# adaLN weights in a two-layer backbone step: 16 of 40 pieces between layer 0's projections, their rows transposed by VectorE

## The chip, the cores and the metric

One core of a Trainium2 chip runs the whole step. The metric is the device time of one execution in microseconds, median of three runs.

## The reference

```python
D_MODEL = 1024; SEQ = 128; DEC_SEQ = 512; DEPTH = 2
def modulation(cvec, w_mod, b_mod):
    m = jax.nn.silu(cvec) @ w_mod + b_mod            # 1024 -> 6 x 1024
    return jnp.split(m[..., None, :], 6, axis=-1)
...
  h = x * (1 + scale1) + shift1                      # adaLN, from c (512 latent tokens) or c_ctx (128 context tokens)
  p = h @ w_in[l]                                    # 1024 -> 3088: q, k, v; gated DeltaNet; HGRN2
  x = LayerNorm(alpha * x + gate1 * (concat(A, B, C) @ w_out[l]))
  x = LayerNorm(alpha * x + gate2 * FFN_l(x * (1 + scale2) + shift2))
```

Each layer needs six vectors of 1024 for each of the two groups, that is, two rows (from c and c_ctx) times a 1024 x 6144 matrix. Only shift1 and scale1 of layer 0 are needed for its projections; the others are read behind its attention.

## The kernel before

The five engines run programs of their own, and semaphores join them. All of w_mod is 48 pieces of 1024 x 256, 1 MB each. Eight of them (layer 0's shift1 and scale1) are loaded first into regions of their own. The other 40 pass through the ring `wbuf`, three slots of 1 MB that SP fills strictly in the order of `weight_plan()`; w_in's pieces pass through the same ring.

**A piece.** `mod_piece_job` on TensorE multiplies it: 8 products over the contraction, with two useful columns of 32 (c and c_ctx) as weights, spread over four groups of 32 PSUM rows. A float32 product is two PE instructions, 16 to a piece. So the piece leaves four partial sums for each of the two rows, at PSUM rows 32q and 32q + 1. `mod_row` on ScalarE copies the 128 x 256 block to `modrow` (four pieces wide). When four are there, `mod_turn` transposes and adds the four partial sums at once: per 128 columns of `modrow` one product with `modrow` as weights and the 128 x 2 matrix `sel` as moving data. `mod_chunk` on VectorE adds the bias and writes `modT`. After the pieces of gate2 of layer 1, `gate_rows` writes those as rows (2 x 1024), which go to memory.

**A piece of w_in** (qa0, qa1, kv, f0, f1, b0, b1, b2, gb, ba, i, gc, qc, in this order) is used in halves of float16. ScalarE's `upper` scales it in its slot (line 1028) and writes the upper half (line 1031), the latter only once the piece two before it, whose region it takes, has been used by TensorE. GpSimd's `lower` (line 804) subtracts and writes the lower half. Only that counts up `w_lo`, on which TensorE's job waits and on which SP's `freed` waits before it refills the slot; a slot that held a piece of w_mod is free when its product is done (`ps_full`). ScalarE calls `upper` for a piece at fixed places between its reads of TensorE's results: f0 behind q3, f1 behind va, b0 and b1 behind f0 and f1, b2 behind b1, gb behind b3, i behind b5, gc behind gb1, qc behind i.

**Order.** The jobs of TensorE take the four PSUM slots in turn, in the order of `psum_plan()`: q0 to q3, ka, va, f0, f1 (each in two parts, a and b), b0 to b5, gb0, gb1, ba, ia, ib, kout, ckt, five rotations `rot`, gc0, gc1, qc0, the first two scores, qc1, and then the attention loop of 20 units x. In unit x TensorE makes the scores of x + 2, transposes the probabilities of x, multiplies two pieces of w_mod, makes the output of x - 1 and, in every second unit, a turn. VectorE makes the scores' maxima of x + 2 and divides x + 1; ScalarE copies the transposed probabilities, exponentiates and copies the output. The rotary products wait for ScalarE's copies of kout and ckt, and VectorE's three operations per rotation run beside GpSimd's `lower` of qc.

```python
                elif what.startswith("mod"):
                    bank, turn = PS[f"{l}.mp{what[3:]}"]
                    sp.wait_ge(ps_full[bank], turn + 1)
                else:
                    sp.wait_ge(sg["w_lo"], SPLIT[f"{l}.{what}"] + 1)
```

Of the kernel before, what the change touches and what calls it, by code (L numbers as in the profile page):

```python
# [55 lines left out]
_WIDTH = [("ident", P), ("sel", 2), ("blk", P), ("rot", P), ("rev", 2 * P), ("am", 5 * P), ("tie", 64), ("mean", 1), ("tile", 17),  # L56
          ("gap", 4), ("hg", 2 * 8 * P), ("room", 2 * 8 * P), ("cos", LAT), ("sin", LAT),
# [10 lines left out]
def constant_table():  # L68
# [50 lines left out]
    put("sel", np.stack([i % 32 == g for g in range(2)], 1))  # L119
# [12 lines left out]

def mod_pieces(x):

    return (2 * x, 2 * x + 1)
# [17 lines left out]
def psum_plan():  # L153
# [4 lines left out]
    for l in range(DEPTH):  # L158
# [3 lines left out]
        j += ["gc0", "gc1", "qc0", "S" + units[0], "S" + units[1], "qc1"]  # L162
        for x in range(len(units)):
# [7 lines left out]
            if l == 0 and x % 2:  # L171
                j.append("*mt" + str(x // 2))
                j += ["g2r"] * (x == 17)
# [48 lines left out]
def weight_plan():  # L222
# [41 lines left out]
def backbone_kernel(nc, x_prompt, x_sample, cache_k, cache_v, state_gdn, state_hgrn, c, c_ctx, w_mod, b_mod, w_in,  # L264
# [12 lines left out]
    with ctx:  # L277
# [142 lines left out]
        rtmp, siluc, g2row = mem(spare, 1024, LAT), mem(spare, 1536, 48), mem(extra, 0, D)  # L420

# [593 lines left out]
        def _(act):  # L1015
# [26 lines left out]
            def mod_row(l, i):  # L1042
                j = f"{l}.mp{i}"
                copy(modrow[:, (i % 4) * 256:(i % 4 + 1) * 256], L.full(j)[:, 0:256], j)


# [13 lines left out]
                       (wr[:, :, :], moe_router[0].rearrange("(k p) e -> p k e", p=P))]  # L1060
            assert len(par_in) == PAR_DMAS
# [4 lines left out]
            for i in range(4):  # L1066
                mod_row(0, i)
# [5 lines left out]
            for i in range(4, 8):  # L1073
                mod_row(0, i)
# [7 lines left out]
            for l in range(DEPTH):  # L1082
# [102 lines left out]
                for x, (n, t) in enumerate(units):  # L1185
# [3 lines left out]
                    if l == 0:  # L1189
                        for i in mod_pieces(x):  # L1190
                            mod_row(*mod_piece(i))
# [7 lines left out]
                    if l == 0 and x == 17:  # L1199
# [457 lines left out]
        def _(dve):  # L1657
# [26 lines left out]
            L.done("par")  # L1684

# [562 lines left out]
        def _(pe):  # L2248
# [107 lines left out]
            for l in range(DEPTH):  # L2356
# [6 lines left out]
                for t in range(2, 4):  # L2363
                    project(l, "qa1", J(f"q{t}"), (t % 2) * P, h2)
# [705 lines left out]
```

## Time and profile before

| | |
|---|---|
| median of 3 runs | 2442.57 us (2441.56 to 2445.93) |
| profiled execution | 2446.07 us, span 2444.3 us, mean granted clock 0.937 |
| PE / DVE / ACT / POOL busy | 2141.7 / 1470.8 / 1284.5 / 758.5 us |
| HBM read / written | 368.35 / 29.11 MB |

Busy times are those of whole engines over stages with different limits; PEld is TensorE's loading of weights. Line 2268 is the helper through which nearly all of TensorE's products go, lines 1662, 1666 and 1670 are VectorE's helpers, and 1020 is ScalarE's copy, so instructions are told apart by their tiles and shapes: `ps<-wbuf,const 128*32 128x256` is the product of a w_mod piece, `ps<-const,modrow 128x2` the turn, `ps<-hT,arena 128x512` a projection job. Line 2475 transposes the probabilities, one group for each unit. SPq is SP's queue of DMA issues. PEclk is the granted clock of TensorE, 1.00 being 2.4 GHz. A row of the windows view gives the stretch, its length, the busy time (x instructions) of PE, PEld, DVE, ACT and POOL, PEclk, the DMA engines' mean share and GB/s. A row of the groups view gives busy us and mean ns of one, then the idle time before them and what ended it.

### The profile page before, as it was taken

What the parts mean: (1) busy time and instruction counts of PE and PEld (TensorE: products, weight loads), DVE (VectorE), ACT (ScalarE), POOL (GpSimd) and SP (SyncE); (2) the same over time, 40 slices, a digit from 0 to 9 for tenths busy, and PEclk for the clock granted to TensorE, in tenths of its full rate; (3) what the DMA queues carried; (4) which work ended last, traced back from release to release, by engine and by line L of the source; (5) the groups of instructions that cost most, each with busy time, mean ns of one, the idle gap of its engine ahead of it and who ended that gap; (6) DMA issues with size and microseconds to landing.
All of it is one profiled execution on the core that took longest, in us unless ns stands there. A gap on an engine that the chain in (4) does not pass through costs nothing.

```text
span 2444.3 us, 54596 instructions
## 1 busy us (share of the span) xinstructions
PE 2141.7 (88%) x23078; PEld 1337.8 (55%) x23078; DVE 1470.8 (60%) x1822; ACT 1284.5 (53%) x1664; POOL 758.5 (31%) x557
## 2 busy tenths in 40 slices
PE   5998987878989999999898878888969999999990
PEld 4765656755565555555765557654544444444440
DVE  3155745559362121214558666486379999999976
ACT  3443753446444242423443764466268787787862
POOL 0432115432314342423232135333123333332321
PEclk8999998888999999999999888889979999999995
DMA  9322990020212222215221000020276677980023
GB/s 277 105 81 76 298 302 11 3 56 4 72 53 72 84 82 73 86 68 162 86 89 38 1 10 3 3 57 22 97 257 207 233 266 275 332 314 35 27 104 137
DMA packets 215386, 278.46 MB, mean 114 GB/s; under 512 B 28178, under 2 KB 188798, under 8 KB 215040
## 3 DMA queue, kind: packets, MB, share of 16 engines
q1 hardware_dynamic: 203776, 243.60, 30.8%
q0 software_dynamic: 8432, 29.89, 3.3%
q8 instruction: 166, 2.72, 0.5%
q10 hardware_dynamic: 2959, 1.83, 0.3%
q14 instruction: 53, 0.43, 0.1%
HBM read 368.35 MB, written 29.11 MB: 163 GB/s over the span
## 4 chain that ended last, share of the span: by engine, by line
PE 52%; issue 16%; DVE 14%; POOL 7%; ACT 6%; DMA 3%; SPq 1%; POOLq 0%; DVEq 0%; ACTq 0%
PE ps L2268 50%; POOL mix L968 5%; DVE arena L1662 2%; DMA wbuf<-in_w_mod 1%; DVE mix L1670 1%; PE ps L2475 1%; DVE xT L1662 1%; DVE const L1662 1%; ACT arena L1142 1%; DVE mix L1662 1%; DVE mix L1666 1%; DVE yg L1662 1%; DVE arena L1666 1%; DVE hT L1662 1%; POOL mix L971 1%
## 5 line engine op out<-in xcount | busy, mean ns | idle before, releaser
L2268 PE MATMUL ps<-hT,mix 128*128 128x512 f16 (+2 forms) x3024 | 377.5, 287 | 24.7 <-DVE hT L1662 15.3
L2268 PE MATMUL ps<-w,xgT 128*128 128x512 f16 x1632 | 365.4, 381 | 7.0 <-DVE w L2163 7.0
L2163 DVE SCALAR_TENSOR_TENSOR w<-wst,w 128x2048 f16<-128x2048 f32 x136 | 309.8, 2317 | 22.8 <-ACT w L1523 22.6
L2268 PEld LDWEIGHTS ps<-hT,mix 128*128 128x128 f16 x3024 | 228.2, 99 | 172.4 <-issue 17.1
L1000 POOL TENSOR_TENSOR a<-aval,a 128x256 f16<-128x256 f32 x68 | 159.1, 2340 | 370.8 <-ACT a L1571 370.8
L2268 PEld LDWEIGHTS ps<-w,xgT 128*128 128x128 f16 x1632 | 157.1, 98 | 185.8 <-issue 10.2
L1523 ACT ACTIVATE w<-wst 128x2048 f16<-128x2048 f32 x136 | 251.5, 1899 | 6.6 <-DMA xs_rows<-htok,slot_i 6.5
L2268 PE MATMUL ps<-mix 128*128 128x512 f16 (+5 forms) x1856 | 204.5, 288 | 14.5 <-POOL mix L971 8.8
L2268 PE MATMUL ps<-hT,arena 128*128 128x128 f16 (+1 forms) x1440 | 201.2, 302 | 1.0 <-DVE const L1662 1.0
L2268 PE MATMUL ps<-w2m,aT 128*128 128x512 f16 x816 | 188.6, 381 | 5.6 <-DVE aT L2201 5.6
L2268 PEld LDWEIGHTS ps<-mix 128*128 128x128 f16 (+3 forms) x1856 | 121.3, 124 | 88.7 <-POOL mix L971 12.4
L2169 DVE SCALAR_TENSOR_TENSOR w2m<-wst,w2m 128x2048 f16<-128x2048 f32 x68 | 155.8, 2291 | 15.8 <-ACT w2m L1531 15.2
L2127 DVE SCALAR_TENSOR_TENSOR mix<-ps,mix 128x640 f32<-128x640 f32 x22 | 18.1, 825 | 239.4 <-PE ps L2268 239.4
L804 POOL TENSOR_TENSOR arena<-wbuf,arena 128x2048 f16<-128x2048 f32 x24 | 100.0, 4166 | 196.1 <-ACT arena L1031 196.0
L2268 PEld LDWEIGHTS ps<-hT,arena 128*128 128x128 f16 x1440 | 112.0, 98 | 88.3 <-issue 5.8
L968 POOL TENSOR_TENSOR mix<-wbuf,mix 128x2048 f16<-128x2048 f32 x33 | 134.2, 4081 | 57.0 <-ACT mix L1475 57.0
L2268 PEld LDWEIGHTS ps<-w2m,aT 128*128 128x128 f16 x816 | 79.8, 98 | 103.1 <-DVE aT L2201 6.4
L2268 PE MATMUL ps<-arena 64*32 64x32 f32 (+5 forms) x4320 | 104.4, 220 | 34.0 <-issue 20.3
L1531 ACT ACTIVATE w2m<-wst 128x2048 f16<-128x2048 f32 x68 | 129.4, 1903 | 0.2 <-PE ps L2268 0.2
L971 POOL TENSOR_TENSOR mix<-mix 128x640 f16<-128x640 f32 x22 | 30.7, 1396 | 258.2 <-ACT mix L1484 258.2
L2134 DVE TENSOR_TENSOR arena<-arena,ps 128x640 f32<-128x640 f32 x80 | 65.6, 821 | 73.7 <-PE ps L2268 73.7
L2268 PEld LDWEIGHTS ps<-arena 64*32 64x32 f32 (+3 forms) x4320 | 70.3, 117 | 66.9 <-issue 43.5
(360 smaller groups left out, 3625.0 us busy)
## 6 DMA issues: line engine op xcount, KB each, us to landing
wst<-in_moe_w SPq DMA_DIRECT2D x204, 1024.0 KB
wbuf<-in_w_mod SPq DMA_DIRECT2D x40, 1024.0 KB
wbuf<-in_ffn_w SPq DMA_DIRECT2D x33, 1024.0 KB
wbuf<-in_w_in SPq DMA_DIRECT2D x20, 1024.0 KB
xs_rows<-in_table SPq DMA_DIRECT2D x17, 512.0 KB, 6.3
ys_rows<-yb POOLq DMA_DIRECT2D x17, 512.0 KB, 4.0
wbuf<-in_w_out SPq DMA_DIRECT2D x32, 256.0 KB
xg<-xs_rows POOLq DMA_DIRECT2D x16, 512.0 KB, 5.7
```

The source lines that it names most:

```text
L804: L.do(g.tensor_tensor(split_parts(what)[1], wpiece(WP[f"{l}.{what}"][0], n), split_parts(what)[0], ALU.subtract), "w_lo")
L968: g.tensor_tensor(v[1], wpiece(j), v[0], ALU.subtract).then_inc(sg["w_lo"], 1)
L971: g.tensor_tensor(a2[1][:, t], gbuf[:, t], a2[0][:, t], ALU.subtract).then_inc(sg["a_lo"], 1)
L1000: g.tensor_tensor(a16[:, s % 2, 1, :], aval[:, s % 2, :], a16[:, s % 2, 0, :], ALU.subtract).then_inc(sg["m_alo"], 1)
L1523: a.activation(quarter(s, p)[0], staged(s, p), ACT.Copy, scale=WS).then_inc(sg["m_hi13"], 1)
L1531: a.activation(w2p[s % 2][0], staged(s, 2), ACT.Copy, scale=WS).then_inc(sg["m_hi2"], 1)
L1662: ins = v_.tensor_tensor(o, x, y, op)
L1666: ins = v_.tensor_scalar(o, x, s1, s2, op0, op1)
L2134: v_.tensor_tensor(yacc[:, m], yacc[:, m], ps[:, b, 0:NT], ALU.add).then_inc(ps_free[b], 1)
L2163: v_.scalar_tensor_tensor(out=q[1], in0=staged(s, p), scalar=WS, in1=q[0], op0=ALU.mult, op1=ALU.subtract).then_inc(sg["m_lo13"], 1)
L2169: v_.scalar_tensor_tensor(out=q[1], in0=staged(s, 2), scalar=WS, in1=q[0], op0=ALU.mult, op1=ALU.subtract).then_inc(sg["m_lo2"], 1)
L2268: return mm_(o, w, x, start=first, stop=last, skip_group_check=True)
```

## The change

- 16 of the 40 pieces get a place in the projections of layer 0 (`MOD_AT`: behind q3, ka, va, f0, f1, b0 to b5, gb0, gb1, i, ckt and gc0), four turns with them (`TURN_AT`). SP fetches them between the pieces of w_in (`MOD_FETCH`). The 24 others are spread over the 20 units, 6 to five units, and their six turns are at `TURN_UNIT`.
- `mod_row` moves from ScalarE to VectorE and becomes a transpose of 32x32 blocks, for all 48 pieces. After it the two rows are columns: in block k of 32 columns they stand at columns 32k and 32k + 1.
- A turn becomes four products, one for each group of 32 output rows, with the wider `sel` (128 x 32) as weights and 16 columns of `modrow` as moving data, in place of eight. `gate_rows` becomes 32 products of 32 columns in place of two of 512.
- `sel` is loaded by a DMA of its own on ScalarE's queue.

```diff
+MOD_AT = {j: i for i, j in enumerate(("q3", "ka", "va", "f0b", "f1b", "b0", "b1", "b2", "b3", "b4", "b5", "gb0", "gb1", "ib",
+                                     "ckt", "gc0"))}
+TURN_AT = {"f1b": 0, "b3": 1, "gb1": 2, "qc0": 3}
+MOD_FETCH = {"f0": (0,), "f1": (1, 2), "b0": (3,), "b1": (4, 5), "b2": (6, 7), "ba": (8, 9), "i": (10, 11), "gc": (12,),
+               "qc": (13, 14, 15)}
+TURN_UNIT = {3: 4, 6: 5, 9: 6, 13: 7, 16: 8, 19: 9}
...
 def mod_pieces(x):
 
-    return (2 * x, 2 * x + 1)
+    return tuple(range(16 + 6 * x // 5, 16 + 6 * (x + 1) // 5))
...
-        j += ["gc0", "gc1", "qc0", "S" + units[0], "S" + units[1], "qc1"]
+        j += ["gc0", "gc1", "qc0"]
+        if l == 0:
+            j = [y for x in j for y in [x] + [f"*mt{TURN_AT[x]}" for _ in "1" if x in TURN_AT]
+                 + [f"*mp{MOD_AT[x]}" for _ in "1" if x in MOD_AT]]
...
-        names += [f"{l}.{x}" for x in j]
+        for x in j:
+            names.append(f"{l}.{x}")
+            if l == 0 and x in MOD_FETCH:
+                names += ["%d.mod%d" % mod_piece(i) for i in MOD_FETCH[x]]
         if l == 0:
-            for i in range(40):
+            for i in range(16, 40):
...
-            def mod_row(l, i):
-                j = f"{l}.mp{i}"
-                copy(modrow[:, (i % 4) * 256:(i % 4 + 1) * 256], L.full(j)[:, 0:256], j)
...
+            o, n = CONST_AT["sel"]
+            par_in.append((sel, table[:, o:o + n]))
...
-            mod_chunk(0, 0)
-            mod_chunk(0, 1)
+            def chunk_of(k):
+                lm, i = mod_piece(4 * k)
+                mod_chunk(lm, i // 4)
+
+            def mod_row(l, i):
+                j = f"{l}.mp{i}"
+                L.free(v_.transpose(modrow[:, (i % 4) * 256:(i % 4 + 1) * 256], L.full(j)[:, 0:256]), j)
+
+            def row_of(job):
+                mod_row(*mod_piece(MOD_AT[job]))
+
+            for c in range(2):
+                for i in range(4):
+                    mod_row(0, 4 * c + i)
+                L.done("par")
+                mod_chunk(0, c)
...
                     modulate(l, 0, 8)
+                    for job in ("q3", "ka", "va"):
+                        row_of(job)
...
+                if l == 0:
+                    row_of("f0b")
                 L.done(J("f1b"))
                 if l == 0:
+                    chunk_of(TURN_AT["f1b"])
+                    row_of("f1b")
...
                 for t in range(6):
+                    if l == 0:
+                        if t == 3:
+                            chunk_of(TURN_AT["b3"])
+                        row_of(f"b{t}")
                     L.done(J(f"b{t}"))
+                    if l == 0 and t == 5:
+                        row_of("gb0")
+                        chunk_of(TURN_AT["gb1"])
+                        row_of("gb1")
...
-                    if l == 0 and x % 2:
-                        lm, i = mod_piece(2 * (x - 1))
-                        mod_chunk(lm, i // 4)
+                    if l == 0:
+                        for i in mod_pieces(x):
+                            mod_row(*mod_piece(i))
+                        if x in TURN_UNIT:
+                            chunk_of(TURN_UNIT[x])
...
                 L.done(f"{l}.mp{4 * c + 3}")
-                for k in range(KT):
-                    ins = mm(s[:, 2 * k:2 * k + 2], modrow[:, k * P:(k + 1) * P], cst("sel"))
+                part = modrow.rearrange("p (k a i) -> p a k i", a=4, i=32)
+                for q in range(4):
+                    ins = mm(s[32 * q:32 * q + 32, 0:16], sel, part[:, q, :, 0:2])
                 close(ins, f"{l}.mt{c}")
 
             def gate_rows():
 
                 s = open_("0.g2r")
-                for h in range(2):
-                    ins = mm(s[0:2, h * 512:h * 512 + 512], cst("sel"), modrow[:, h * 512:h * 512 + 512])
+                for k in range(32):
+                    ins = mm(s[0:2, k * 32:k * 32 + 32], modrow[:, k * 32:k * 32 + 2], sel)
...
+                def mods_at(job):
+                    if l:
+                        return
+                    if job in TURN_AT:
+                        lm, i = mod_piece(4 * TURN_AT[job])
+                        mod_turn(lm, i // 4)
+                    if job in MOD_AT:
+                        mod_piece_job(*mod_piece(MOD_AT[job]))
+
                 for t in range(2, 4):
                     project(l, "qa1", J(f"q{t}"), (t % 2) * P, h2)
+                mods_at("q3")
                 project(l, "kv", J("ka"), 0, h2)
+                mods_at("ka")
```

The order of SP's loads, from the load of f0 on. Rows with `in_w_in` are pieces of w_in, 128x2048 is a table. Before:

```order
L700 DMA wbuf<-in_w_in 128x8x256 [waits w_lo] x5
L643 DMA const<-in_table 128x2048 [waits ps_full2]
L700 DMA wbuf<-in_w_in 128x8x256 [waits w_lo]
L700 DMA wbuf<-in_w_in 128x8x16 [waits w_lo]
L700 DMA wbuf<-in_w_in 128x8x256 [waits w_lo] x3
```

and with the change, as far as the load of b2, the table and two pieces behind them:

```order
L716 DMA wbuf<-in_w_in 128x8x256 [waits w_lo]
L716 DMA wbuf<-in_w_mod 128x8x256 [waits w_lo]
L716 DMA wbuf<-in_w_in 128x8x256 [waits w_lo]
L716 DMA wbuf<-in_w_mod 128x8x256 [waits w_lo]
L716 DMA wbuf<-in_w_mod 128x8x256 [waits ps_full1]
L716 DMA wbuf<-in_w_in 128x8x256 [waits w_lo]
L716 DMA wbuf<-in_w_mod 128x8x256 [waits ps_full3]
L716 DMA wbuf<-in_w_in 128x8x256 [waits ps_full1]
L716 DMA wbuf<-in_w_mod 128x8x256 [waits w_lo]
L716 DMA wbuf<-in_w_mod 128x8x256 [waits ps_full0]
L716 DMA wbuf<-in_w_in 128x8x256 [waits w_lo]
L659 DMA const<-in_table 128x2048 [waits ps_full2]
```

The pieces of w_mod (M0 to M15 in the order of their use) now take slots between those of w_in: M0 behind f0; M1, M2 behind f1; M3 behind b0; M4, M5 behind b1; M6, M7 behind b2 and the table; M8, M9 behind gb and ba; M10, M11 behind i; M12 behind gc; M13, M14, M15 behind qc.

TensorE from the job va (128x128, 120 products) to turn 0. Before:

```order
L2268 MATMUL ps<-arena,hT 128x128 [waits ps_free2,w_lo]
L2268 MATMUL ps<-arena,hT 128x128 x119
L2268 MATMUL ps<-arena,hT 128x256 [waits ps_free3,w_lo]
L2268 MATMUL ps<-arena,hT 128x256 x95
L2268 MATMUL ps<-arena,hT 128x256 [waits ps_free0]
L2268 MATMUL ps<-arena,hT 128x256 x23
```

and with the change, from M1 on:

```order
L2308 MATMUL ps<-wbuf,const 32x256 [waits ps_free3,w_full0]
L2308 MATMUL ps<-wbuf,const 32x256 x7
L2308 MATMUL ps<-arena,hT 128x128 [waits ps_free0,w_lo]
L2308 MATMUL ps<-arena,hT 128x128 x119
L2308 MATMUL ps<-wbuf,const 32x256 [waits ps_free1,w_full1]
L2308 MATMUL ps<-wbuf,const 32x256 x7
L2308 MATMUL ps<-arena,hT 128x256 [waits ps_free2,w_lo]
L2308 MATMUL ps<-arena,hT 128x256 x95
L2308 MATMUL ps<-arena,hT 128x256 [waits ps_free3]
L2308 MATMUL ps<-arena,hT 128x256 x23
L2308 MATMUL ps<-wbuf,const 32x256 [waits ps_free0,w_full0]
L2308 MATMUL ps<-wbuf,const 32x256 x7
```

Each product of a piece stands in TensorE's queue between two projection jobs and waits there for its own transfer (`w_full`).

## Rows read from the trace of the kernel before

**Rows 1.** Windows view, five stretches: length, then the columns as told above.
```profile
71.20:193.80 122.60, 122.60 (x1131) 86.47 (x1132) 43.56 (x41) 50.98 (x49) 43.20 (x14) 0.99 0.32 101
239.30:268.80 29.50, 25.71 (x267) 16.79 (x267) 19.70 (x41) 20.40 (x44) 2.87 (x8) 0.88 0.86 273
268.80:304.10 35.30, 35.30 (x385) 24.88 (x385) 26.19 (x60) 25.99 (x56) 4.73 (x10) 1.00 0.93 296
304.10:335.20 31.10, 30.28 (x352) 21.01 (x350) 17.92 (x50) 19.71 (x50) 3.16 (x10) 0.95 0.99 314
335.20:371.50 36.30, 29.38 (x284) 17.51 (x283) 8.88 (x38) 14.57 (x45) 4.48 (x13) 0.84 0.79 254
```

**Rows 2.** Waits of PE, 239.3 to 371.5 us: total us, times, longest.
```profile
PE ps L2268 <- DMA wbuf<-in_w_mod: 8.1, 8, 2.4
PE ps L2475 <- DVE arena L1666: 5.8, 2, 4.2
```

**Rows 3.** Groups by form, 0 to 380 us: busy us, mean ns | idle before.
```profile
L2268 PE MATMUL ps<-wbuf,const 128*32 128x256 f32 x640 | 45.3, 421 | 8.1 <-DMA wbuf<-in_w_mod 8.1
L2268 PE MATMUL ps<-const,modrow 128*128 128x2 f32 x192 | 26.6, 269 | 1.0 <-ACT modrow L1020 0.9
L1020 ACT ACTIVATE modrow<-ps 128x256 f32<-128x256 f32 x48 | 18.4, 383 | 41.2 <-PE ps L2268 40.6
```

**Rows 4.** Timeline of PE, ACT and SP, 84 to 125 us: start, us.
```profile
84.23 6.68 PE L2268 MATMUL ps<-hT,arena 128*128 128x512 f16 x48
84.49 0.70 ACT L1020 ACTIVATE arena<-ps 128x640 f32<-128x640 f32 x1 [5.82 <-PE ps L2268]
90.75 33.06 PE L2268 MATMUL ps<-arena,hT 128*128 128x128 f16 x360
93.32 0.39 SPq L700 DMA_DIRECT2D wbuf<-in_w_in  x1
97.70 0.70 ACT L1020 ACTIVATE va<-ps 128x640 f32<-128x640 f32 x1 [6.00 <-PE ps L2268]
```

**Rows 5.** GB/s in 40 slices: 92 to 102, then 105 to 121 us.
```profile
GB/s 0 0 0 0 0 0 0 0 0 29 49 147 168 266 295 352 385 393 385 389 385 389 340 172 115 0 0 0 0 0 0 0 0 0 0 0 0 0 0 0
...
GB/s 0 0 0 0 0 0 31 97 248 356 384 374 381 392 463 407 430 410 430 410 389 82 0 0 0 0 0 0 0 0 0 0 0 0 0 0 0 0 56 108
```

**Rows 6.** Timeline at the rotations, 193 to 206 us, PE and DVE.
```profile
198.44 4.54 PE L2268 MATMUL ps<-arena,const 128*128 128x512 f32 x6 [2.79 <-ACT koutb L1020]
198.56 4.43 DVE L1662 TENSOR_TENSOR arena<-arena,const 128x512 f32<-128x512 f32 x1
```

**Rows 7.** Timeline of PE around 240 us, then its window to 243.7.
```profile
232.26 1.93 PE L2268 MATMUL ps<-wbuf,const 128*32 128x256 f32 x32
239.29 0.87 PE L2475 MATMUL ps<-const,arena 128*128 128x128 f32 x6 [4.24 <-DVE arena L1666]
240.10 3.60 PE L2268 MATMUL ps<-wbuf,const 128*32 128x256 f32 x32
...
240.00:243.70 3.70, 3.70 (x36) 1.55 (x36) 2.85 (x9) 1.19 (x2) 0.00 (x0) 0.54 0.38 103
```

**Rows 8.** Timeline of PE, short float32 products at 391 us.
```profile
391.14 1.15 PE L2268 MATMUL ps<-arena,extra 64*64 64x64 f32 x32 [0.85 <-ACT arena L1249]
```

**Rows 9.** Timeline of PE, the second turn of the prologue.
```profile
37.44 2.29 PE L2268 MATMUL ps<-const,modrow 128*128 128x2 f32 x16 [0.66 <-ACT modrow L1020]
```

**Rows 10.** Timeline of DVE in a unit of the attention loop.
```profile
277.03 1.23 DVE L1670 SCALAR_TENSOR_TENSOR arena<-ps,const 128x1024 f32<-128x1024 f32 x1 [0.51 <-PE ps L2268]
278.29 1.22 DVE L1858 TENSOR_REDUCE small<-arena 128x2 f32<-128x1024 f32 x1
...
283.29 1.23 DVE L1670 SCALAR_TENSOR_TENSOR arena<-ps,const 128x1024 f32<-128x1024 f32 x1 [0.89 <-PE ps L2268]
```

**Rows 11.** Groups of DVE by form, 0 to 380 us.
```profile
L1666 DVE TENSOR_SCALAR arena<-ps 128x256 f32<-128x256 f32 x4 | 1.7, 425 | 4.1 <-PE ps L2268 4.1
L1790 DVE RECIPROCAL lbt<-extra 128x512 f32<-128x512 f32 x1 | 3.4, 3353 | 0.0
```

More of the change, by code:

```diff
@@ L53 @@
 OFF_BA, OFF_F, OFF_I, OFF_QC, OFF_GC, OFF_GB, OFF_B, OFF_KV = 1792, 1808, 2320, 2576, 2832, 1536, 768, 512
-_WIDTH = [("ident", P), ("sel", 2), ("blk", P), ("rot", P), ("rev", 2 * P), ("am", 5 * P), ("tie", 64), ("mean", 1), ("tile", 17),
-          ("gap", 4), ("hg", 2 * 8 * P), ("room", 2 * 8 * P), ("cos", LAT), ("sin", LAT),
+_WIDTH = [("ident", P), ("skip", 2), ("blk", P), ("rot", P), ("rev", 2 * P), ("am", 5 * P), ("tie", 64), ("mean", 1), ("tile", 17),
+          ("gap", 4), ("hg", 2 * 8 * P), ("room", 2 * 8 * P), ("cos", LAT), ("sin", LAT), ("sel", 32),
           ("zero", D), ("near", 2 * 6 * 32), ("wide", 4 * 2 * 64), ("first", 3 * 64)]
@@ L118, in constant_table @@
     put("tie", np.broadcast_to((e[None, :] < e[:, None]).reshape(1, 64), (P, 64)))
-    put("sel", np.stack([i % 32 == g for g in range(2)], 1))
+    put("sel", np.stack([i % 32 == g for g in range(32)], 1))
     put("tile", np.broadcast_to(np.arange(MT).reshape(1, MT), (P, MT)))
@@ L161, in psum_plan @@
         j += ["gb0", "gb1", "ba", "ia", "ib", "kout", "ckt"] + [f"rot{t}" for t in range(5)]
-        j += ["gc0", "gc1", "qc0", "S" + units[0], "S" + units[1], "qc1"]
+        j += ["gc0", "gc1", "qc0"]
+        if l == 0:
+            j = [y for x in j for y in [x] + [f"*mt{TURN_AT[x]}" for _ in "1" if x in TURN_AT]
+                 + [f"*mp{MOD_AT[x]}" for _ in "1" if x in MOD_AT]]
+        j += ["S" + units[0], "S" + units[1], "qc1"]
         for x in range(len(units)):
@@ L170, in psum_plan @@
                 j.append("O" + units[x - 1])
-            if l == 0 and x % 2:
-                j.append("*mt" + str(x // 2))
-                j += ["g2r"] * (x == 17)
+            if l == 0 and x in TURN_UNIT:
+                j.append("*mt" + str(TURN_UNIT[x]))
+                j += ["g2r"] * (x == 16)
             j += SIDE.get(x, [])
@@ L1065, in _ @@
                                 L.full("cT")[:, 0:16].rearrange("p (g k) -> p g k", g=2), ACT.Silu), "cT")
-            for i in range(4):
-                mod_row(0, i)
             s = L.full("par")
@@ L1072, in _ @@
             upper(0, "qa0")
-            for i in range(4, 8):
-                mod_row(0, i)
             tokens_in(0)
@@ L1198, in _ @@
                     side(x)
-                    if l == 0 and x == 17:
+                    if l == 0 and x == 16:
                         copy(g2row[0:2, :], L.full("0.g2r")[0:2, :], "0.g2r")
@@ L1833, in _ @@
                 stt(SP, ZA, -1.0, ZA, ALU.mult, ALU.max, to="ab_in")
+                if l == 0:
+                    row_of("ib")
+                    row_of("ckt")
                 dve.wait_ge(sg["rope_in"], 16 * (l + 1))
@@ L1840, in _ @@
                     tt(qk[:, t, 0:LAT], qk[:, t, 0:LAT], rtmp, ALU.add, to="rope_ready")
+                if l == 0:
+                    row_of("gc0")
+                    chunk_of(TURN_AT["qc0"])
                 def scores(x):
@@ L1905, in _ @@
                         divide(x + 1)
-                    if l == 0 and x % 2:
-                        lm, i = mod_piece(2 * (x - 1))
-                        mod_chunk(lm, i // 4)
+                    if l == 0:
+                        for i in mod_pieces(x):
+                            mod_row(*mod_piece(i))
+                        if x in TURN_UNIT:
+                            chunk_of(TURN_UNIT[x])
                     side(x)
@@ L2379, in _ @@
                 tokens(J("va"), w, (P, 256), range(TT))
+                mods_at("va")
                 for p_ in ("f0", "f1"):
@@ L2391, in _ @@
                 tokens(J("ib"), w, (0, 256), range(4, 5))
+                mods_at("ib")
                 L.done(J("ka"))
@@ L2402, in _ @@
                     project(l, "gc", J(f"gc{t}"), t * P, h2)
+                    mods_at(f"gc{t}")
                 project(l, "qc", J("qc0"), 0, h2)
+                mods_at("qc0")
                 L.need("rope_ready", 5)
@@ L2481, in _ @@
                         output(x - 1)
-                    if l == 0 and x % 2:
-                        lm, i = mod_piece(2 * (x - 1))
+                    if l == 0 and x in TURN_UNIT:
+                        lm, i = mod_piece(4 * TURN_UNIT[x])
                         mod_turn(lm, i // 4)
-                    if l == 0 and x == 17:
+                    if l == 0 and x == 16:
                         gate_rows()
```

11 lines of the change are left out of this document (6 added, 5 removed).

## The prediction

> **What bounds the kernel now.** I first cut the span by the busy time of each engine in stretches [rows 1]. From 71.2 to 193.8 us, layer 0's projections, PE is busy in all of 122.6 us at a granted clock of 0.99 while DMA is used for 0.32 of the time. From 239.3 to 371.5 us, the attention loop, PE is still busy 88 to 100% of three of the four stretches, but DMA is at 0.86 to 0.99: the 40 pieces of w_mod pass here, two to a unit. Then I asked for the waits [rows 2]: in the whole loop PE idles only 8.1 us for w_mod and 5.8 us for VectorE. So the loop is not bound by DMA alone: most of what the pieces cost is PE's own time, 45.3 us for 40 products (1.13 us each) and 26.6 us for 12 turns (2.2 each) [rows 3]. Moving a piece to the projections moves its product from one busy stretch of PE to another and gains nothing by itself. The gain must come from the shorter turns and the waits; what the move breaks is the supply of weights.
>
> I count against the profiled execution, 2446.07 us with a span of 2444.3; the median of the three runs is 2442.57, 3.5 lower. I take the difference that I work out and put it on the median. About 0.2%, 4.9 us, is what a measurement of this kernel can tell from no change.
>
> **The projections, product by product.** M0 to M15 are the moved products. A pair of products takes 1.93 us at full clock [rows 7], so 16 take 15.5 us, and PE has no idle time there to hide them in: +15.5. Four short turns replace nothing here. One is 8 PE instructions; the nearest row has 32 short ones in 1.15 us [rows 8], 0.29 for 8, the lower end; the long turn's 2.2 is the upper. I take 0.4, near the short row: +1.6.
>
> Now the waits. The ring wbuf has three slots and SP fills them strictly in order. A slot of a w_in piece comes free only when POOL has written its lower half. For f0 the row of the trace is: PE begins the job after q3 at 84.23, ACT reads q3 at 84.49, then splits f0, POOL subtracts, and SP issues at 93.32 [rows 4]: **9.1 us from the end of the PE job to the issue**. The transfer starts then; the bandwidth line goes to zero at 98.25, 4.9 us after the issue, and with two transfers in line 7.3 us after it [rows 5], so 2.4 for each further one. A projection job takes 6.5 us (84.23 to 90.75), a half of f 13.2 (33.06 for va and the two halves; va ends some 0.3 before ACT reads it at 97.70, so it is 6.7) [rows 4]. With the SP order of the change:
> - M1 sits in the slot of f0, freed 9.1 after q3. It lands at 14.0; PE asks after M0 and ka, 1.0 + 6.5. Wait 6.5.
> - M3 stands behind b0, and b0 takes the slot of f1, freed 9.1 after va: 16.4 against M2 and f0, 14.1. Wait 2.3.
> - M6 stands behind b2 and the 1 MB table load; the slot is b1's, freed 9.1 after f1: 18.8 against turn 0, M4, b0, M5, b1, 15.4. Wait 3.4.
> - M9 sits in the slot of gb, freed 9.1 after b3: 14.0 against turn 1, M8 and b4, 7.9. Wait 6.1.
> - M12 stands behind gc, in the slot of i, freed 9.1 after b5: 16.4 against 15.4. Wait 1.0.
>
> The other eleven come in time by the same sums. Together +19.3. Behind a waiting M stands everything of PE; the weights' chain through ACT and POOL is released by PE's jobs, so it is late as well and gives nothing back.
>
> The clock. After 4.24 us of idle PE ran a pair of products in 3.60 instead of 1.93 us, at a granted clock of 0.54 in that stretch [rows 7]: almost all of it at the lower level, 1.2 GHz. That is 1.7 us lost per such idle. M1, M6 and M9 give idles of that size: +5.1. (Lower end 0; upper end in the rivals.)
>
> Around the rotations M13 and M14 fall into a wait that PE has anyway, 2.79 us for ACT's koutb copy [rows 6]: -1.9. But VectorE comes to the rotations later against POOL's 4 us subtraction, and its product of two SBUF operands took 4.43 us there [rows 6]; the second rotation's bank comes free about 1.5 us later: +1.5. In the prologue the turn of chunk 1 stands on the path, 2.29 us [rows 9], now 0.4, and the table for it adds one small DMA: -1.7 with the transpose's 0.2 over the copy counted in. ScalarE loses 48 copies of 383 ns [rows 3]; it waited for PE before 40.6 us of them, so that is worth nothing here. The prologue's rows now wait on VectorE for tab_in, but w_mod for them lands later than that anyway (PE's turn of [rows 9] comes at 37.44, right behind the last of them).
>
> Sum: 15.5 + 1.6 + 19.3 + 5.1 - 0.4 - 1.7 = **+39.4 us**.
>
> **The attention loop.** Unit 0 has one piece less, -1.1. For the rest I take each stretch of [rows 1] twice: PE's busy time less the pieces (1.13) and turns that go, and VectorE's busy time plus 0.03 for each instruction (277.03 + 1.23 to 278.29 in [rows 10]) plus 0.45 for each transpose. A transpose is not in the trace. A 128x256 operation from PSUM takes 425 ns, the slowest kind of instruction 3.35 us for 512 columns [rows 11], 1.7 for 256: I take 0.42 and a gap, the nearest row. (The Trainium skill, Vector Engine (DVE) Microarchitecture Reference, 3.8, has the transpose sustain one element per cycle and lane, which at the 0.96 GHz of VectorE: DVE Perf Modes, Specifications, is an estimate of 0.27 us; by it the loop would gain 3 us more.)
> - 239.3 to 268.8, units 1 to 4, 8 pieces become 5, two turns one: PE 18.3, VectorE 19.7 + 1.2 + 2.3 = 23.2. They hand work to each other, I take 25.0: -4.5.
> - 268.8 to 304.1, units 5 to 9, 10 become 6, three turns two: PE 25.0, VectorE 26.2 + 1.8 + 2.7 = 30.7: -4.6. **VectorE becomes the bound.** In a unit of 6.26 us it has only 0.89 us idle even now [rows 10].
> - 304.1 to 335.2: PE 21.8, VectorE 22.1; 23.0: -8.1.
> - 335.2 to 371.5: PE 29.4 - 4.5 - 5.8 = 19.1, plus 1.0 because the gate rows become 64 short instructions (64 x 0.036 = 2.3 at least, at a long turn's 2.2 / 16 = 0.14 apiece 8.8 at most; I take 2.9 against 1.9), plus 1.0 of waits; 21.1: -15.2. Here the w_mod waits of [rows 2] go, since 6 pieces for five units leave DMA ahead.
>
> Sum: **-33.5 us**. Net +5.9 us, 2446.07 to 2452.0, on the median **2448.5 us**.
>
> **Rivals.**
> 1. VectorE's transposes fall into its idle time and PE alone sets the loop. For: it idles in every unit [rows 10]. Against: the idle is 0.9 us and operand hand-overs use it. PE 18.3 + 25.0 + 21.8 + 20.1 and the 5.8 us of [rows 2] make 91.0 instead of 132.2, with unit 0 -42.3; net -2.9, 2439.7. Chance 0.24.
> 2. The pieces land before PE asks, because the issue comes sooner than 9.1 us after the job. Then the 19.3 and the 5.1 fall away: net -18.5, **2424**, faster. It decides at M1: if it lands within 7.5 us of q3. Against: [rows 4] has ACT and POOL in a row between. Chance 0.10.
> 3. The clock falls at all five new waits and stays low twice as long: 5 x 3.4 instead of 5.1, +11.9, 2460. For: the row of 0.54 came after a wait of just this kind of length. Against: two of the five are shorter than 2.5 us, and the projections around them are dense. This is also what the Trainium skill, TensorE: Matmul & The Clock Gate, "HAM oscillation", says against this change: DMA waits between matmuls put the array back on the lower clock each time; by that rule the time is this rival's 2460, and the row of 0.54 agrees with it. Chance 0.12.
> 4. The transpose runs like the slowest instruction, 1.7 us: 1.25 more for each of 17 in the first three stretches, where VectorE is the bound, +21, 2470. Against: no arithmetic in it. Chance 0.07.
>
> The forecast itself has 0.47, with a range of its own from 2441 to 2455. That the change doesn't take place is excluded by the instruction order.
>
> **How the numbers follow.** Faster by over 4.9 us: rival 2 and a third of rival 1, 0.18. Same: most of the rest of rival 1 and a third of the forecast, 0.29. Slower: 0.53. The range 2433 to 2462 holds the forecast, rival 1 with the loop 7 us better than I make it, and rival 3; it leaves out rivals 2 and 4.
>
> **What would show it.** Right: PE waits for wbuf before the products after ka and after b4, 5 to 7 us each, and shorter ones after f0 and b1; the first score of layer 0 some 39 us later than at 222.5; a granted clock under 0.99 in the projections; in the loop VectorE over 85% busy in units 5 to 9, and hardly a w_mod wait; the first product of the next stage within some 6 us of 371.5. Wrong: no wait at the product after ka, or a transpose far from 0.4 us, or the loop from unit 1 on no longer than rival 1's 91 us, where I forecast 132.2 - 32.4 = 99.8.

## The result and the profile after

| | before | after |
|---|---|---|
| median (4 runs each, side by side) | 2442.07 us | **2478.39 us** (2477.10 to 2480.81) |
| ratio, 95% interval | | 1.0147 [1.0131, 1.0163] |
| profiled execution, span | 2446.07, 2444.3 | 2477.10, 2475.3 |
| PE / DVE / ACT busy | 2141.7 / 1470.8 / 1284.5 | 2131.5 / 1493.6 / 1266.0 |

Slower, as forecast, but by 36 us where 6 were forecast, and outside the range. The times here and below are those of fast executions: one of e7 (3643.69 us) and one of e8 (3610.20 us), both at a mean granted clock of 0.55, are left out. In the changed kernel lines 2308, 2535, 1668, 1672, 1036 and 820 are what 2268, 2475, 1662, 1666, 1020 and 804 were; 1789 is the transpose of a row.

I laid four landmarks of PE beside each other: the start of `q2` (71.17 before), the first score of layer 0 (222.47), the first product of the stage behind the loop (371.51) and the end of the span.

| from, to | before | after | difference | forecast |
|---|---|---|---|---|
| start to `q2` | 71.2 | 70.3 | -0.9 | -1.7 |
| `q2` to the first score | 151.3 | 202.7 | +51.4 | +41.1 |
| first score to the end of the loop | 149.0 | 123.5 | -25.5 | -33.5 |
| behind the loop | 2072.8 | 2078.8 | +6.0 | 0 |

First the projections: waits of PE from 70.3 to 273.0 us (total us, times, longest), and in PE's timeline the rows at the first two of them; the last four rows are SP's queue of DMA issues.

```profile
PE ps L2308 <- DMA wbuf<-in_w_mod: 24.4, 5, 6.9
PE ps L2308 <- ACT koutb L1036: 1.3, 1, 1.3
```

```profile
83.41 1.07 PE L2308 MATMUL ps<-wbuf,const 128*32 128x256 f32 x16
84.42 6.69 PE L2308 MATMUL ps<-hT,arena 128*128 128x512 f16 x48
97.69 1.94 PE L2308 MATMUL ps<-wbuf,const 128*32 128x256 f32 x16 [6.58 <-DMA wbuf<-in_w_mod]
99.56 8.81 PE L2308 MATMUL ps<-arena,hT 128*128 128x128 f16 x120
108.31 1.07 PE L2308 MATMUL ps<-wbuf,const 128*32 128x256 f32 x16
127.06 1.50 PE L2308 MATMUL ps<-wbuf,const 128*32 128x256 f32 x16 [4.48 <-DMA wbuf<-in_w_mod]
...
92.40 1.02 SPq L716 DMA_DIRECT2D wbuf<-in_w_mod  x2
117.30 0.39 SPq L716 DMA_DIRECT2D wbuf<-in_w_in  x1
117.73 0.58 SPq L716 DMA_DIRECT2D wbuf<-in_w_mod  x1
118.36 1.22 SPq L716 DMA_DIRECT2D wbuf<-in_w_in  x1
```

`q3` ends where M0 starts, at 83.41; SP issues M1 at 92.40, 9.0 us later ([rows 4] gave 9.1), and PE stands still for it until 97.69. Before the change no product waited there. Behind the wait M1 takes 1.94 us and the job after it 8.81 us, where the same forms take 1.07 and (in [rows 4]) about 6.7. The granted clock from 97.7 to 107.0 us is 0.68. The five waits are 6.58, 4.48, 4.23, 6.91 and 2.22 us, before M1, M3, M6, M9 and M12, the very five of the forecast.

Then the loop, cut at the same units as [rows 1] (windows view, columns as there), and its waits (answering to [rows 2]).

```profile
289.80:316.30 26.50, 21.14 (x195) 13.22 (x195) 21.93 (x44) 17.71 (x37) 5.33 (x8) 0.78 0.53 169
316.30:351.30 35.00, 28.47 (x288) 18.40 (x288) 29.07 (x66) 21.82 (x43) 4.07 (x10) 0.95 0.57 183
351.30:375.80 24.50, 21.78 (x267) 15.07 (x263) 20.43 (x53) 15.92 (x41) 3.78 (x10) 1.00 0.68 218
375.80:396.50 20.70, 15.79 (x248) 9.71 (x246) 11.63 (x43) 10.70 (x34) 4.39 (x13) 1.00 0.74 239
```

```profile
PE ps L2308 <- DVE modrow L1789: 9.0, 5, 3.4
PE ps L2535 <- DVE arena L1672: 6.1, 2, 5.1
PE ps L2535 <- DVE modrow L1789: 3.7, 4, 2.1
PE ps L2535 <- ACT arena L1036: 3.0, 1, 3.0
PE ps L2308 <- DMA wbuf<-in_w_mod: 1.3, 1, 1.3
```

```profile
L1789 DVE STREAM_TRANSPOSE modrow<-ps 128x256 f32<-128x256 f32 x48 | 21.6, 450 | 101.7 <-PE ps L2308 100.8
L2308 PE MATMUL ps<-modrow,const 128*32 128x16 f32 x96 | 3.2, 196 | 10.4 <-DVE modrow L1789 10.4
```

The waits for w_mod are nearly gone (1.3 for 8.1) and twelve turns take 3.2 us for 26.6 [rows 3]. In their place PE waits 12.7 us for VectorE's transposed rows: 9.0 at the turns and 3.7 for PSUM banks that only the transpose sets free. Units 5 to 9 take 35.0 us, as long as before with four pieces more.

### The profile page after: what moved, and what is told of

It reads as the page before. It is cut to its first block, busy times and chain, and to the rows that moved or that the text cites. A ratio compares the mean times of both kernels' runs of the same rounds, so it can differ in the third digit from the quotient of the medians.

```text
span 2475.3 us, 54524 instructions
## 1 busy us (share of the span) xinstructions
PE 2131.5 (86%) x23042; PEld 1321.5 (53%) x23042; DVE 1493.6 (60%) x1870; ACT 1266.0 (51%) x1616; POOL 755.4 (31%) x557
## 4 chain that ended last, share of the span: by engine, by line
PE 47%; DVE 17%; issue 16%; POOL 8%; ACT 7%; DMA 3%; SPq 1%; POOLq 0%; DVEq 0%; ACTq 0%
PE ps L2308 45%; POOL mix L984 5%; DVE arena L1668 2%; DMA wbuf<-in_w_mod 2%; DVE mix L1676 1%; DVE arena L1672 1%; DVE mix L1668 1%; POOL arena L820 1%; DVE xT L1668 1%; ACT arena L1151 1%; DVE const L1668 1%; DVE mix L1672 1%; DVE hT L1668 1%; DVE yg L1668 1%; SPq L716 1%
## 5 line engine op out<-in xcount | busy, mean ns | idle before, releaser
L2308 PEld LDWEIGHTS ps<-mix 128*128 128x128 f16 (+3 forms) x1856 | 122.3, 125 | 90.4 <-POOL mix L987 12.4
L987 POOL TENSOR_TENSOR mix<-mix 128x640 f16<-128x640 f32 x22 | 30.7, 1397 | 258.2 <-ACT mix L1490 258.2
```

Of the source, the lines that this page charges most:

```text
L987: g.tensor_tensor(a2[1][:, t], gbuf[:, t], a2[0][:, t], ALU.subtract).then_inc(sg["a_lo"], 1)
L2308: return mm_(o, w, x, start=first, stop=last, skip_group_check=True)
```

## The experiments

The runs came in three groups, e1 to e4, e5 to e8 and e9 to e11. The kernel before, run beside each group, had medians of 2446.17, 2445.63 and 2443.49 us; ratios are against it, and kernels of different groups are compared by their distance from it. Four theories were at hand: the waits in the projections with the clock behind them (W, C), VectorE's rows (V), and, for the 6 us behind the loop, where no instruction had changed, the place of the code in PE's program (Q) or chance. The diffs show the lines that matter; calls on VectorE that only follow a moved job are left out.

### e1: the rows without the move

```diff
-MOD_AT = {"q3": 0, "ka": 1, ... "gc0": 15}
+MOD_AT = {}
-    return tuple(range(16 + 6 * x // 5, 16 + 6 * (x + 1) // 5))
+    return (2 * x, 2 * x + 1)
```

> No piece is moved: all 40 stay in the attention loop, and only the transposing by VectorE and the four short products are kept. Theory W (what the change lost is the waits for w_mod tiles among the projections, 24 us, and the lower clock behind them, about 10 us): without moved pieces both are gone, the first score starts within 1 us of where it did before the change, and the loop's turns give back some of 26.6 us of PE time less the waits for VectorE's rows (13.5 us in the changed kernel with 24 pieces, so 15 to 22 us with 40): 2430 to 2440. Rival V (VectorE's rows themselves are the loss, by the PSUM banks and turns that they hold up): slower than before, 2450 or more. Rival H (the 5 us that appeared behind the loop belong to the new code): 2445.

Measured: **2449.81 us, 1.0023 [1.0005, 1.0041]**. W's 2430 to 2440 is missed, and V's 2450 nearly met. The waits among the projections are gone (first score at 218.27, 4.2 us earlier than before the change, 2.4 of them ahead of the projections), yet the loop takes 152.9 us against 149.0 and ends at 371.15, where it ended before (371.51). The waits of that loop, and the window of its last units, say why:

```profile
PE ps L2286 <- DMA wbuf<-in_w_mod: 11.2, 7, 2.9
PE ps L2286 <- DVE modrow L1787: 8.6, 9, 2.0
PE ps L2286 <- ACT arena L1034: 2.2, 1, 2.2
PE ps L2513 <- DVE modrow L1787: 2.1, 1, 2.1
```

```profile
263.70:371.20 107.50, 87.66 (x1013) 53.38 (x1014) 67.03 (x178) 48.46 (x117) 11.94 (x32) 0.88 0.85 273
```

PE is busy for 122.6 us of that loop instead of 133.2, so the turns do save 10.6 us; the waits for w_mod rise from 8.1 to 11.2 and those for rows from 0.3 (behind ScalarE's copies) to 10.7. What PE saves it spends waiting, in part for weights (DMA at 0.85 in the later units), in part for VectorE. That short turns pay only if pieces leave the loop is argued from this, not shown: no run has all 40 pieces there with the rows ahead of the division (e3). What e1 loses against the kernel before lies behind the loop (2082.5 us for 2072.8), where theory H had put something; e9 returns to it.

### e2: the move with long turns

```diff
-                L.free(v_.transpose(modrow[...], L.full(j)[:, 0:256]), j)
+                L.free(v_.tensor_copy(modrow[...], L.full(j)[:, 0:256]), j)
-                for q in range(4):
-                    ins = mm(s[32 * q:32 * q + 32, 0:16], sel, part[:, q, :, 0:2])
+                for k in range(KT):
+                    ins = mm(s[:, 2 * k:2 * k + 2], modrow[:, k * P:(k + 1) * P], sel[:, 0:2])
```

> The pieces move as in the change, but the rows are copied by VectorE without a transpose and turned by the eight long products (and two for the gate rows) of the kernel before. Theory W: the waits for w_mod tiles stay as they are, 24 to 26 us, the turns cost about 1.7 us more each, ten in all, and the waits of PE for VectorE's rows stay, since a copy of the same tile is as long (425 ns in the row of before): 2478 + 17 = 2490 to 2497. Rival V (the transposes are what VectorE is late with): the waits for rows vanish, 13.5 us, and the time is 2478 to 2484.

Measured: **2491.71 us, 1.0201 [1.0167, 1.0235]**. W's number. In the loop PE waits 9.6 and 1.3 us for rows that are merely copied (424 ns each against 450 for the transpose), so V as a matter of the transpose falls: it is the hand-over to VectorE that costs, whatever VectorE does to the row. The w_mod waits were 19.9 us, less than the 24 to 26 expected. No run moves the pieces and leaves the rows to ScalarE; that it is VectorE's hand-over rests on this run and on e1's 10.7 us for 0.3.

### e3: the rows ahead of the division

```diff
-                    if x + 1 < len(units):
-                        divide(x + 1)
                     if l == 0:
                         for i in mod_pieces(x):
                             mod_row(*mod_piece(i))
+                    if x + 1 < len(units):
+                        divide(x + 1)
```

> The change, but in the attention loop VectorE transposes the rows of a unit's pieces ahead of the next unit's division, not behind it. Theory: PE's waits for rows (9.8 us at the turns, 3.7 us for a PSUM bank) shrink to under 4 us, and the loop gets 5 to 10 us shorter: 2468 to 2474. Rival: the division then comes later by two transposes (0.9 us) in each unit and PE waits for it in place of the rows: 2476 to 2482. Nothing changes ahead of the first score.

Measured: **2468.81 us, 1.0102 [1.0069, 1.0135]**. The loop takes 118.5 us for 123.5. Its waits, and the window of units 5 to 9:

```profile
PE ps L2536 <- DVE arena L1672: 14.0, 9, 5.6
PE ps L2309 <- DVE modrow L1789: 2.8, 4, 1.0
...
314.40:345.70 31.30, 28.39 (x288) 18.56 (x288) 28.48 (x62) 21.81 (x43) 3.64 (x10) 0.95 0.56 182
```

Both sides of the expectation hold at once: the waits for rows fall to 2.8 us and those for the division rise from 6.1 to 14.0. What is left is mostly VectorE's own time: units 5 to 9 take 31.3 us, with VectorE busy for 28.48 of them, near the 30.7 that the forecast had for a VectorE that never waits.

### e4: every moved piece one job later

```diff
-MOD_AT = {"q3": 0, "ka": 1, "va": 2, "f0b": 3, "f1b": 4, ... "gc0": 15}
-TURN_AT = {"f1b": 0, "b3": 1, "gb1": 2, "qc0": 3}
+MOD_AT = {"q3": 0, "va": 1, "f0b": 2, "f1b": 3, "b0": 4, ... "gc1": 15}
+TURN_AT = {"b0": 0, "b4": 1, "ib": 2, "qc0": 3}
```

> Every moved piece is multiplied one job of the projections later than in the change, with its transfer issued where it was. Theory W: each transfer has one more job (6.5 to 13 us) to land in, longer than the longest wait (6.9 us), so the six waits of 25.8 us shrink to under 3 us, the clock stays up where they stood (about 10 us more), and the first score starts 30 to 34 us earlier than in the change: 2440 to 2450. Rival P (PE's own time for the moved products and the tiles' share of the DMA queues is the loss, the waits only a sign of it): the waits turn up at other jobs or the projections' own weights are late instead, 2465 or more. Rival C (waits go, but the clock falls as much without them): 2450 to 2458.

M0 stays where it was, and the turns come later with their pieces.

Measured: **2439.81 us, 0.9977 [0.9959, 0.9994]**: 0.2% faster than before the change. PE does not wait for w_mod once between `q2` and the first score, which starts at 241.06 instead of 273.00, 31.9 us earlier. Windows from `q2` to the first score, of the change and of e4:

```profile
70.30:273.00 202.70, 175.08 (x1573) 110.01 (x1573) 68.75 (x77) 61.88 (x59) 48.87 (x18) 0.92 0.47 150
```

```profile
70.90:241.10 170.20, 167.00 (x1574) 106.15 (x1574) 65.95 (x77) 61.98 (x59) 50.65 (x18) 0.98 0.56 179
```

The same instructions, 8.1 us less of busy PE at a clock of 0.98 for 0.92, and 24.4 us less of waiting. Theory W stands; P falls, since the same tiles moved through the same queue and nothing else came late.

### e7: PE kept busy in the waits

```diff
                 s = open_(f"{l}.mp{i}")
+                for k in range({(0, 9): 27, (0, 11): 18, (0, 14): 17, (0, 17): 29, (0, 20): 7}.get((l, i), 0)):
+                    mm(s[0:32, 0:512], h2[0][:, 0, 0:32], h2[0][:, 0, 0:512])
+                w = piece(f"{l}.mod{i}")
```

> The change, with f16 products on 512 columns written to the waiting piece's own PSUM bank ahead of its wait: 27, 18, 17, 29 and 7 at the five waits for w_mod (6.6, 4.5, 4.2, 6.9, 2.2 us), overwritten by the piece. The waits' ends stay, since the tiles land when they land; only PE's idling goes. Theory C (10 us are lost at the lower clock after the waits, because PE had stood still): the clock stays at its higher level, the pieces and products behind the waits run at 1.07 and 6.69 us, and the first score starts 7 to 10 us earlier than 273.0; about 2468 to 2472. Rival T (the slow products behind the waits come from the tiles or weights that land at that time, not from the clock): nothing changes or it gets later by the overshoot, 2478 to 2482.

Measured: **2466.40 us (three executions), 1.0080 [1.0050, 1.0111]**. PE's timeline at M1:

```profile
97.91 1.07 PE L2308 MATMUL ps<-wbuf,const 128*32 128x256 f32 x16 [0.58 <-DMA wbuf<-in_w_mod]
98.91 6.87 PE L2308 MATMUL ps<-arena,hT 128*128 128x128 f16 x120
```

```profile
70.50:264.60 194.10, 187.70 (x1672) 115.31 (x1672) 68.85 (x77) 62.03 (x59) 48.89 (x18) 0.98 0.49 157
```

M1 still starts when its tile lands (97.91 for 97.69), but then it takes 1.07 us for 1.94, and the job behind it 6.87 for 8.81. The granted clock from `q2` to the first score is 0.98, and the first score starts at 264.56, **8.4 us earlier** than in the change. That is the price of the lower clock behind five waits, shown apart from the waits themselves; T falls. Against e4's 241.06 the remaining 23.5 us are the waits. The median, 12 us under the change's, says less: the 98 added products also stand ahead of the stretch that e5 and e8 are about.

### e5, e8: 36 records more in PE's program, in the loop or behind

e5 repeats three of the four short products in each of the loop's six turns, on e4; e8 puts 36 small products into e4 behind the stretch in question, at layer 0's fourth output projection.

```diff
-                for q in range(4):
+                for q in ((1, 2, 3) if l else ()) + (0, 1, 2, 3):
                     ins = mm(s[32 * q:32 * q + 32, 0:16], sel, part[:, q, :, 0:2])
```

```diff
                     open_(J(f"wo{m}"))
+                    if l == 0 and m == 3:
+                        w = split_piece(l, "wo1")
+                        for k in range(36):
+                            mm(ps[:, PS[J("wo3")][0]][:, 0:32], w[0][:, 0, P:2 * P], mixed(0, 0)[:, 0:32], True, True)
```

> The kernel with every moved piece one job later, and 18 repeated short products (36 records and 36 weight loads) spread over the loop's six turns, so that PE's program counts as many instructions behind the loop as before the change. Theory Q (the stretch of small products behind the attention loop, where PE stands still 'for nothing that the profile shows', depends on where its instructions lie in PE's program: 5.6 us of such waits before the change and 5.3 with the long turns, both with 23078 matmul records; 8.8 to 13.0 in the four kernels with 23042): the waits in that stretch fall from 9.5 to about 5.5 us at the same products as before the change, the added products cost 1 us, and the time is 4 to 7 us below the same kernel without them: 2432 to 2437. Rival (chance, or the time that passed before): 9 us of such waits stay and the time is 2440 to 2442.

> Every moved piece one job later, and 36 small products added behind the stretch of small products, in the output projection of layer 0. Theory Q (place in PE's program): the stretch itself lies as without them, its unexplained waits stay at 9.5 us, and the time is that of the kernel without them or up to 2 us more: 2440 to 2443. Rival (the total count of PE's instructions or the length of the program decides, wherever they stand): 2433 to 2437, as with the products in the loop.

Measured: e5 **2431.02 us, 0.9955 [0.9938, 0.9971]**; e8 **2441.61 us, 0.9986 [0.9973, 0.9998]**. As many records added ahead of the stretch made the kernel 8 us faster against e4 (14.6 for 6.4 us under the kernel before) and 10.6 against e8, which ran beside it; added behind it, they gave nothing. Q stands and its rival falls.

### e9, e10: the same on the change itself, and the change once more

> The change with nothing but the 18 repeated short products in the loop's turns. Theory Q (place of the small products in PE's program): the unexplained waits in the stretch behind the loop fall from 8.8 to about 5.5 us and stand at the products where they stood before the change; with the first score at 273 and the end of the loop at about 397 as in the change, the time is 4 to 9 us below the change run beside it: about 2470. Rival (that gain belonged to pieces that land in time): no difference from the change.

> The changed kernel itself on this chip, profiled once more. By place in the program its unexplained waits behind the loop come at the same products again, and their sum is 8 to 10 us; the waits for w_mod tiles are 23 to 27 us in six. If the waits behind the loop were chance, they come elsewhere or sum up to 5 us. Time: 2476 to 2484.

Measured: e9 **2467.07 us, 1.0101 [1.0085, 1.0118]**; e10 **2478.51 us, 1.0151 [1.0134, 1.0169]**. Eleven microseconds from 18 products that compute nothing new. In e10 the waits for w_mod are 25.8 us in six, as expected. "issue" is idle time for which the profile shows no cause. Waits of PE over the same 3500 products, from the 2000th to the 5500th behind the end of the loop, which is some 114 to 317 us behind it (the sums in the expectations are over a shorter stretch): the kernel before, the change, e9.

```profile
PE ps L2268 <- issue: 12.4, 10, 4.0
```

```profile
PE ps L2308 <- issue: 16.3, 14, 4.6
```

```profile
PE ps L2308 <- issue: 12.3, 11, 3.7
```

The other kernels with 23078 matmul records have 12.4 (e2), 12.8 (e5) and 12.7 us (e6, below); those whose program is short by 36 records at this place have 15.8 to 18.5 (e1, e3, e4, e8, e10). Other counts give other sums: 8.8 us in e7, with 98 records more than the change ahead of the stretch, and 10.6 in e11, with 72 more. The waits stand mostly at the same products within each family. PE's timelines: the kernel before, then e9, then the change, then e10.

```profile
599.23 0.31 PE L2268 MATMUL ps<-arena 64*32 64x32 f32 x22 [0.54 <-issue]
602.70 0.25 PE L2268 MATMUL ps<-arena 64*32 64x32 f32 x6 [0.76 <-issue]
```

```profile
614.70 0.31 PE L2308 MATMUL ps<-arena 64*32 64x32 f32 x22 [0.26 <-issue]
618.44 0.25 PE L2308 MATMUL ps<-arena 64*32 64x32 f32 x6 [0.92 <-issue]
```

```profile
628.44 0.26 PE L2308 MATMUL ps<-mix 64*32 64x32 f32 x6 [0.81 <-issue]
632.50 0.25 PE L2308 MATMUL ps<-arena 64*32 64x32 f32 x3 [0.98 <-issue]
```

```profile
624.66 0.26 PE L2308 MATMUL ps<-mix 64*32 64x32 f32 x6 [1.09 <-issue]
628.44 0.25 PE L2308 MATMUL ps<-arena 64*32 64x32 f32 x3 [0.70 <-issue]
```

Before x22 and x6 in the first two, before another x6 and x3 in the last two. Counted from the start of PE's program these are one and the same pair of places: in all four kernels the pauses come after exactly 7636 and 7763 matmul records. The traces have more such places. Of the 13 kernels 10 pause for over 0.3 us after exactly 6244 records, 10 after 6624 and 12 after 7763, and the distances between 6244, 6624, 7130, 7636 and 7763 are multiples of 126 to 127. The change had made all of PE's later program 36 products and 36 weight loads shorter, so other products came to stand there. That it is the loading of the program is likely but not shown: the profile of the change has a queue of kind "instruction" that moves 2.70 MB in 165 packets, and each of the eight pauses that it has at this spacing from 6244 to 7763 begins 0.7 to 2.3 us after the start of such a packet.

The pauses are not the whole size. Windows over the same 3500 products: e4, e5, e10, e9.

```profile
477.50:686.20 208.70, 177.03 (x3508) 109.92 (x3503) 112.43 (x164) 107.06 (x201) 71.50 (x59) 0.87 0.19 49
475.70:674.30 198.60, 168.75 (x3508) 105.22 (x3503) 112.19 (x164) 107.00 (x201) 73.10 (x59) 0.90 0.19 52
```

```profile
505.30:711.40 206.10, 171.46 (x3507) 107.77 (x3504) 112.88 (x164) 107.04 (x201) 71.72 (x59) 0.90 0.19 50
504.50:703.00 198.50, 169.82 (x3507) 106.00 (x3502) 112.51 (x164) 106.92 (x201) 73.04 (x59) 0.90 0.19 52
```

From e4 to e5 the stretch loses 10.1 us: pauses give 3.7 of them, and PE is busy for 8.3 us less, at a granted clock of 0.90 for 0.87. From e10 to e9 it loses 7.6 us: 4.2 of pauses, 1.6 of busy PE, the rest of waits for other engines. The stretch takes 195.2 to 199.1 us in the five kernels that have the full count of records ahead of it (before, e2, e5, e6, e9), and 204.0 to 211.1 in the six that are short by 36. Over the whole kernel the pauses hardly fall, from 35.9 to 35.5 us (e4, e5) and from 39.1 to 37.2 (e10, e9): their sum does not tell the time. In e7 the stretch has the fewest pauses, and all that lies behind the loop still takes 2080.5 us, for 2078.8 in the change and 2068.6 in e9.

### e6, e11: the pieces put together

e6 is e4 with e3's order and e5's products; e11 has six added products for each turn of the loop in place of three.

```diff
-                for q in ((1, 2, 3) if l else ()) + (0, 1, 2, 3):
+                for q in ((0, 1, 2, 3, 2, 3) if l else ()) + (0, 1, 2, 3):
```

> The same kernel and, with it, VectorE's rows ahead of the next unit's division. In the changed kernel that brought the loop 5.1 us (123.5 to 118.5) and the whole about 9: expected 4 to 6 us below the run with the added products alone, 2427 to 2433. Rival: with the pieces landed in time the division has less slack and PE waits for it instead: no gain.

> As the best kernel so far (pieces one job later, rows early, 36 added records), with 72 added records in place of 36. Theory Q: the waits behind the loop move to other products once more and their sum changes by some us in either direction (the four places tried so far gave 5.3 to 13.0); the added products themselves cost 1 us. Rival (36 was no special number, any padding helps, by slowing the loop): the time stays at 2429 to 2431.

Measured: e6 **2429.46 us, 0.9943 [0.9926, 0.9961]**, the fastest kernel here, 0.6% under the kernel before; e11 **2436.87 us, 0.9968 [0.9957, 0.9979]**. e6 ends its loop at 360.14 against 362.64 in e5, but the medians differ by 1.6 us, less than can be told. In e11 the pauses of that stretch are 10.6 us and those of the whole kernel 41.7 against 35.4 in e6: padding is no remedy that goes one way, it shifts pauses elsewhere too. The same padding in the kernel before was not run.

## Why the prediction was wrong

The direction held, and so did the five waits and VectorE as the bound of units 5 to 9. The time was 29.9 us off, 2478.4 against 2448.5. The largest step that failed is one that the sum doesn't have: the stage behind the loop stands in it at nothing and holds some 11 of the 29.9 us. The next is the loop with 8.0, then the waits with 5.1, the clock with 3.3 and PE's own work with 2.7, all on the same side. Step by step:

- **Waits in the projections, said +19.3, measured +24.4.** The chain of 9.1 us from job to issue was right to 0.1 us, and M1 (6.58 for 6.5) and M9 (6.91 for 6.1) with it. M3 was off by 2.2 (4.48 for 2.3), M6 by 0.8, M12 by 1.2. For M3 I counted 7.3 us from the issue of the first of two transfers in line [rows 5]. In the trace `b1` was issued right behind it, and M3 was there 9.3 us after its own issue. Counting what is queued ahead of a transfer was not enough here. That the transfer queued behind M3 made it later is a guess from this one row.
- **The clock, said +5.1, measured +8.4 (e7).** All five waits were followed by slow products, not only the three that I had counted: behind 2.22 us of waiting M12 took 1.40 us for 1.07. Rival 3's "all five" was right, its "twice as long" (17 us) was not. The rule of the Trainium skill that I set beside it (TensorE: Matmul & The Clock Gate, "HAM oscillation") describes DMA waits of about 3 to 5 us between matmuls, each of which puts the array back on the lower clock. The trace agrees on the four waits of 4.23 us and more, and e7 and e4 bear it out from the other side; the 2.22 us wait is shorter than the page's. My 2460 was more than the page gives, since two of the five waits that I forecast were 2.3 and 1.0 us.
- **PE's own work ahead of the first score, said +15.0, measured 50.5 - 24.4 - 8.4 = +17.7.** e4, without waits, has 18.6. The prologue gave 0.9 for the 1.7 that I had, and around the rotations PE waited 1.30 and 1.90 us (for ACT and for VectorE) where 2.79 had stood, +0.4 for -0.4.
- **The loop, said -33.5, measured -25.5.** A transpose took 0.45 us, as taken. (I wrote that the trace showed none. It has one, beyond the stretch that I had asked for: 50 of 128x512 between SBUF tiles, 711 ns each.) By stretches: unit 0 was no shorter (said -1.1), units 1 to 4 took 26.5 (said 25.0), 5 to 9 **35.0 (said 30.7)**, 10 to 14 24.5 (said 23.0), the rest 20.7 (said 21.1). The step that failed is the one for units 5 to 9: I took the sum of VectorE's busy time as the time of the stretch. Its busy time was right (29.07 us for 28.9), but that is 0.83 of the 35.0. In VectorE's program the rows stand behind the next unit's division; while they wait PE stands before a turn or a bank, and then VectorE waits for PE. e3, which changes only that order, comes to 31.3.
- **Behind the loop, said 0, measured +6.0 between the profiles and, as what is left of the medians, about 11** (29.9 less 5.1, 3.3, 2.7 and 8.0 above). Of the 4.8 us between the two, 3.5 are there because the profiled run of before stood above its median and 1.3 because that of the change stood below; that they fall behind the loop is not shown. I had costed a program shorter by 36 records at nothing there, without a reason. e5, e8 and e9 show that 36 records more ahead of the stretch of small products give 8 to 11 us back.
- **The rivals.** 1 (PE alone sets the loop) fell: PE waited 12.7 us for rows. 2 (the tiles land in time) did not happen in the change, but e4 makes it happen: with the clock up and no waits the kernel is 6 us faster than before and with the added products 14.6, where I had 18.5. 3 (the clock) is above. 4 (transposes of 1.7 us) fell at 0.45.

Summed up, the waits cost 24.4 us, their clock 8.4, PE's own work ahead of the first score 17.7 and the stage behind the loop about 11; the loop gave back 25.5. That is the 36 us. e4 takes away the waits and their clock, and ends its loop 32.2 us earlier (364.30 for 396.54). Its median lies 38.7 under e10's; the 6 us between the two figures are not explained (between the profiled runs of e4 and the change it is 28.7, and that of e4 was the slowest of its ten).

## What to carry to other kernels

Work moved into a stretch where one engine is always busy brings at least its own time with it (here 17.7 us for 15.5 of products); what decides then is whether its operands are there. Place it by the time from the event that frees its buffer to the landing of the transfer: here one job later was the difference between 1.5% slower and 0.2% faster. Where a wait can't be avoided, count the slow products behind it too. Handing a copy from ScalarE to a VectorE that works through a chain made its consumer wait for the chain, not for the 0.45 us of the copy. And a change of the number of instructions has a price of its own further on, here 8 to 11 us for 36 records; look at stretches that the change doesn't touch.

## What was not expected of the hardware

- Idle PE costs twice: five waits of 24.4 us together cost 8.4 us more in slower products, all of which 98 discarded products (f16, 512 columns) gave back (e7).
- The time of a stretch of mostly small float32 products (64x32) depends on where it lies in PE's program: with 36 matmul records more or fewer ahead of it 3500 products took 195.2 to 199.1 or 204.0 to 211.1 us. Most of the unexplained pauses in it (12.3 to 12.8 or 15.8 to 18.5 us together) come after fixed counts of records from the start of the program, some 126.5 apart, whatever product stands there, and mostly repeated when the same kernel ran again. Part of the rest is granted clock (0.87 and 0.90 in e4 and e5). What makes the pauses stays open.
